# Expert weight stream of a two-layer trunk: VectorE's side steps placed further back, a later second scatter, and the first eight weight pieces loaded early

## The reference, cut to what matters

```python
def swiglu(h, w1, w3, w2):
    return jnp.matmul(jax.nn.silu(jnp.matmul(h, w1)) * jnp.matmul(h, w3), w2)

def moe_swiglu(h, router, w1, w3, w2):
    logits = jnp.einsum('bld,de->ble', h, router, preferred_element_type=F32)
    top_v, top_i = lax.top_k(logits, TOP_K)                       # TOP_K = 2, N_EXPERTS = 8
    wts = jax.nn.softmax(top_v, axis=-1)
    gates = jnp.sum(jax.nn.one_hot(top_i, N_EXPERTS, dtype=F32) * wts[..., None], axis=-2)
    y = jnp.zeros_like(h)
    for e in range(N_EXPERTS):
        y = y + gates[..., e:e + 1].astype(h.dtype) * swiglu(h, w1[e], w3[e], w2[e])
    return y
```

## Time and profile before

| | us |
|---|---|
| median of 3 runs | 2085.04 |
| lowest, highest | 2084.29, 2087.69 |
| the profiled execution | 2080.13 |
| its span, first to last instruction | 2078.3 |

### The profile page before, as it was taken

One profiled execution on the slowest core, in us unless ns is written; L12 is line 12 of the kernel. 1 busy time (PEld: TensorE's weight loads), 2 busy tenths in 40 slices (PEclk: granted clock), 3 DMA queues, 4 the chain that ended last, 5 costly groups with the idle time before them and its releaser, 6 DMA issues.

```text
span 2078.3 us, 34564 instructions
## 1 busy us (share of the span) xinstructions
PE 1870.7 (90%) x15227; PEld 1214.5 (58%) x15227; DVE 1169.4 (56%) x1387; ACT 346.5 (17%) x615; POOL 72.8 (4%) x60
## 2 busy tenths in 40 slices
PE   4999999986799999697899996779999999999997
PEld 1334556985444444243546586476868768687684
DVE  2130154764533222122133476489989998998996
ACT  2001144002232222111012402211010000100000
POOL 0032000001000000000050000000000000000000
PEclk9999999757899999799999976789999999999999
DMA  9631210001245544321122100099999999999993
GB/s 341 260 122 61 81 41 0 1 1 41 106 144 196 199 145 182 122 97 46 41 81 101 41 1 20 21 367 411 412 412 410 401 410 396 402 408 397 410 400 139
DMA packets 112803, 408.88 MB, mean 197 GB/s; under 512 B 13880, under 2 KB 20728, under 8 KB 106512
## 3 DMA queue, kind: packets, MB, share of 16 engines
q1 hardware_dynamic: 110608, 405.60, 50.4%
q10 hardware_dynamic: 2048, 1.02, 0.2%
HBM read 405.55 MB, written 1.05 MB: 196 GB/s over the span
## 4 chain that ended last, share of the span: by engine, by line
PE 71%; DVE 18%; issue 4%; DMA 3%; ACT 2%; DVEq 1%; SPq 1%; POOLq 0%; PEldq 0%; ACTq 0%; POOL 0%; PEld 0%
DVE ARENA L1641 12%; PE PS L1259 11%; PE PS L602 11%; PE PS L600 8%; PE PS L1241 6%; PE PS L814 5%; PE PS L1523 4%; PE PS L1526 4%; PE PS L1525 4%; PE PS L1178 3%; PE PS L447 2%; PE PS L1071 2%; PE PS L1545 1%; DMA ARENA<-in_ada_w 1%; PE PS L1503 1%
## 5 line engine op out<-in xcount | busy, mean ns | idle before, releaser
L1641 DVE TENSOR_TENSOR ARENA<-ARENA 128x2816 bf16<-128x2816 f32 (+1 forms) x192 | 581.5, 3083 | 5.6 <-DMA ARENA<-in_moe_w 3.7
L1523 PE MATMUL PS<-ARENA 128*128 128x96 bf16 x2816 | 375.5, 209 | 41.8 <-DVE ARENA L1641 37.0
L1526 PE MATMUL PS<-ARENA 128*128 128x96 bf16 x2816 | 374.7, 208 | 0.1
L1525 PE MATMUL PS<-ARENA 128*128 128x96 bf16 x2816 | 374.7, 208 | 0.0
L1523 PEld LDWEIGHTS PS<-ARENA 128*128 128x128 bf16 x2816 | 279.4, 99 | 56.5 <-DVE ARENA L1641 48.8
L1525 PEld LDWEIGHTS PS<-ARENA 128*128 128x128 bf16 x2816 | 279.6, 99 | 5.3 <-issue 5.3
L1526 PEld LDWEIGHTS PS<-ARENA 128*128 128x128 bf16 x2816 | 279.4, 99 | 0.5 <-issue 0.3
L1545 PE MATMUL PS<-ARENA 128*96 128x512 bf16 x1056 | 237.6, 384 | 3.1 <-DVE ARENA L1641 3.1
L602 PE MATMUL PS<-ARENA 128*128 128x512 f32 (+1 forms) x608 | 237.4, 536 | 2.4 <-ACTq L397 2.4
L1259 PE MATMUL PS<-ARENA 128*128 128x512 bf16 x1056 | 232.4, 381 | 2.4 <-DVE ARENA L1291 2.4
L380 DVE TENSOR_TENSOR ARENA<-ARENA 128x4096 bf16<-128x4096 f32 (+1 forms) x26 | 91.4, 3522 | 226.8 <-ACT ARENA L374 226.8
(11 more groups left out here) (222 smaller groups left out, 1574.6 us busy)
## 6 DMA issues: line engine op xcount, KB each, us to landing
ARENA<-in_moe_w SPq DMA_DIRECT2D x128, 1408.0 KB, 13.4
ARENA<-in_moe_w SPq DMA_DIRECT2D x48, 1536.0 KB, 16.3
ARENA<-in_ada_w SPq DMA_DIRECT2D x24, 2048.0 KB, 7.8
ARENA<-in_ffn_w SPq DMA_DIRECT2D x15, 2048.0 KB, 7.8
ARENA<-in_w_in SPq DMA_DIRECT2D x12, 2048.0 KB, 8.0
ARENA<-in_moe_w SPq DMA_DIRECT2D x16, 1024.0 KB, 16.7
ARENA<-in_w_out SPq DMA_DIRECT2D x8, 1024.0 KB, 5.6
ARENA<-in_w_in SPq DMA_DIRECT2D x4, 1024.0 KB, 6.1
```

The source lines that it names most:

```text
L1523: pe.matmul(out, hi[:, f:f + P], HEH[:, k, :], start=k == 0 and b % 4 == 0, stop=False, skip_group_check=True)
L1525: pe.matmul(out, hi[:, f:f + P], HEL[:, k, :], start=False, stop=False, skip_group_check=True)
L1526: mm = pe.matmul(out, lo[:, f:f + P], HEH[:, k, :], start=False, stop=k == KC - 1, skip_group_check=True)
L1641: dve.tensor_tensor(WLO[q % NSLOT][:, 0:n], RAW[q % NSLOT][:, 0:n], WHI[q % NSLOT][:, 0:n], ALU.subtract).then_inc(S("m_lo"), 1)
```

## The change

The weight slots and the small tiles of the experts get other places in the arena, so that six of the eight slots lie where nothing is live once the states stage of layer 1 is over. `MIXB`, an output of the states stage, moves away from one of these places. The tiles of the two halves, formerly one tile each with a half index, are now two tiles; shapes and types of the instructions stay.

SP doesn't wait for stage 12 any more but for stage 10 (states). Before its loop it issues pieces 0 to 7 of the first expert: PE opens six slots at the end of its states stage in layer 1 and the last two at the start of `pe_moe_first`. In the loop, SP issues pieces 8 to 23 of an expert and then 0 to 7 of the next; after the last expert of a round it issues pieces 0 to 7 of expert 0 once more, for a round that may follow. With one round those eight loads are used by nobody.

DVE's side steps move: the addition of x = 0 from split 3 to 7, of x = 1 from 6 to 14, the products of the first half from 9 to 11, the one-hot matrices from 12 to 14, the products of the second half from 17 to 18, and the token steps from 20 to 22. PE's scatter of x = 1 moves from after piece 3 to after piece 8. `m_w2_next` is counted by SP and waited for by nobody.

```diff
@@
-        MIXB = A(116, NT, 512)
+        MIXB = A(16, NT, 512)
@@
-        RAW = [A(12 * s, 3 * D) for s in range(NSLOT)]
+        RAW = [A(at, 3 * D) for at in (40, 52, 64, 76, 96, 108, 0, 12)]
+        EARLY = 6
-        WLO = [A(96 + 6 * s, 3 * D // 2).bitcast(BF16) for s in range(NSLOT)]
+        WLO = [A(at, 3 * D // 2).bitcast(BF16) for at in (24, 30, 88, 120, 126, 132, 138, 144)]
...
+        def sp_piece(sp, i, e, q):
+            sp_slot_free(sp, i, q)
+            if q == 16:
+                sp.sem_inc(S("m_w2_next"), 1)
...
+            sp.dma_start(dst, src).then_inc(S(f"m_raw{q % NSLOT}"), 16)
+
         def sp_moe(sp):
             for other in ENG:
-                sp.wait_ge(S(f"{other}_stage_done"), MOE_STAGE)
...
+                sp.wait_ge(S(f"{other}_stage_done"), EARLY_STAGE)
+            for q in range(NSLOT):
+                sp_piece(sp, 0, 0, q)
+            n = sp.value_load(NROUND[0:1, 0:1], min_val=1, max_val=NROUNDS)
+            with sp.Fori(0, n) as c:
+                with sp.Fori(0, N_EXP - 1) as e:
+                    i, later = sp.snap(c * N_EXP + e), sp.snap(e + 1)
+                    for q in range(NSLOT, NPIECE):
+                        sp_piece(sp, i, e, q)
+                    for q in range(NSLOT):
+                        sp_piece(sp, i + 1, later, q)
+                for q in range(NSLOT, NPIECE):
+                    sp_piece(sp, c * N_EXP + N_EXP - 1, N_EXP - 1, q)
+                for q in range(NSLOT):
+                    sp_piece(sp, c * N_EXP + N_EXP, 0, q)
@@
         def pe_moe_first(pe):
-            pe.sem_inc(S("m_used"), USED)
+            pe.sem_inc(S("m_used"), NSLOT - EARLY)
@@
-                    if q == 3:
-                        pe.wait_ge(S("m_added"), 4 * i + 2)
-                        pe_scatter(pe, 1)
...
                 for q in range(8, 12):
                     uv_piece(i, q, UBANK)
+                    if q == 8:
+                        pe.wait_ge(S("m_added"), 4 * i + 2)
+                        pe_scatter(pe, 1)
@@
-                    if q == 3:
+                    if q == 7:
                         dve_add(dve, 0, 4 * i)
-                    if q == 6:
+                    if q == 11:
+                        dve_hidden(dve, i, 0)
+                    if q == 14:
                         dve_add(dve, 1, 4 * i + 2)
-                    if q == 9:
-                        dve_hidden(dve, i, 0)
-                    if q == 12:
                         dve_onehot(dve, i + 1)
...
-                    if q == 17:
+                    if q == 18:
                         dve_hidden(dve, i, 1)
-                    if q == 20:
+                    if q == 22:
                         dve.wait_ge(S("m_gt"), i + 1)
@@
-        MOE_STAGE = 12
+        EARLY_STAGE = 10
@@
                     stage(pe, L)
+                    if L == 1 and stage == pe_states:
+                        pe.sem_inc(S("m_used"), USED - NSLOT + EARLY)
```

More of the change, by code:

```diff
@@ L1334, in trunk @@
         HALF, HB = D_FF // 2, FC // 2
-        RAW = [A(12 * s, 3 * D) for s in range(NSLOT)]
+        RAW = [A(at, 3 * D) for at in (40, 52, 64, 76, 96, 108, 0, 12)]
+        EARLY = 6
         WHI = [v.bitcast(BF16).rearrange("p (n two) -> p n two", two=2)[:, :, 1] for v in RAW]
-        WLO = [A(96 + 6 * s, 3 * D // 2).bitcast(BF16) for s in range(NSLOT)]
[L1338 to L1343, removed]
+        WLO = [A(at, 3 * D // 2).bitcast(BF16) for at in (24, 30, 88, 120, 126, 132, 138, 144)]
+        UA = [A(150, HB * SLOTS), A(154.125, HB * SLOTS)]
+        AEH = [v.bitcast(BF16).rearrange("p (n two) -> p n two", two=2)[:, :, 1] for v in UA]
+        AEL = [A(158.25, HB * SLOTS // 2).bitcast(BF16), A(36, HB * SLOTS // 2).bitcast(BF16)]
+        HEH, HEL = [A(at, KC * SLOTS // 2).bitcast(BF16).rearrange("p (k s) -> p k s", k=KC) for at in (38.0625, 94)]
+        PG = [A(39.5625, SLOTS), A(95.5, SLOTS)]
         MOLD = BYTES
@@ L1467, in sp_slot_free @@
                 sp.wait_ge(S("m_used"), USED * i + USED + 3 * (q // 4 - 2) + q % 4 + 1)
+        def sp_piece(sp, i, e, q):
+            sp_slot_free(sp, i, q)
+            if q == 16:
+                sp.sem_inc(S("m_w2_next"), 1)
+            if q < 16:
+                half, k = q // 8, 2 * (q % 4)
+                w = t["moe_w3" if q % 8 >= 4 else "moe_w1"][0, bass.ds(e, 1), P * k:P * k + 2 * P,
+                                                           HALF * half:HALF * half + HALF]
+                src = w.rearrange("a (k p) n -> p (a k) n", p=P)
+                dst = RAW[q % NSLOT][:, 0:2 * HALF].rearrange("p (k n) -> p k n", k=2)
+            else:
+                c0, c1 = YBLOCKS[q - 16]
+                w = t["moe_w2"][0, bass.ds(e, 1), P * c0:P * c1, :]
+                src = w.rearrange("a (c p) n -> p (a c) n", p=P)
+                dst = RAW[q % NSLOT][:, 0:D * (c1 - c0)].rearrange("p (c n) -> p c n", n=D)
+            sp.dma_start(dst, src).then_inc(S(f"m_raw{q % NSLOT}"), 16)
@@ L1540, in y_piece @@
                     half, s0 = c // HB, SLOTS * (c % HB)
-                    ah, al = AEH[:, half, s0:s0 + SLOTS], AEL[:, half, s0:s0 + SLOTS]
+                    ah, al = AEH[half][:, s0:s0 + SLOTS], AEL[half][:, s0:s0 + SLOTS]
                     for h in range(2):
@@ L1604, in act_silu_u @@
                 act.wait_ge(S("m_full"), FULL * i + 6 * half + n + 1)
-                act.activation(UA[:, half, SLOTS * b0:SLOTS * b1], B(UBANK + n)[:, 0:SLOTS * (b1 - b0)],
+                act.activation(UA[half][:, SLOTS * b0:SLOTS * b1], B(UBANK + n)[:, 0:SLOTS * (b1 - b0)],
                                ACT.Silu).then_inc(S("m_u"), 1)
```

9 lines of the change are left out of this document (4 added, 5 removed).

## The result

| | before | after |
|---|---|---|
| median (runs) | 2085.26 us (6) | 2075.97 us (6) |
| lowest, highest | 2082.90, 2087.69 | 2069.56, 2076.70 |
| the profiled execution, its span | 2080.13, 2078.3 | 2076.63, 2074.9 |

The ratio is 0.9949, with a 95% interval from 0.9935 to 0.9963: faster by about 10 us, where 2070 was forecast with a range of 2059 to 2080. A second set of runs of the same changed kernel gave 0.9952 (0.9939 to 0.9966).

The account below looks back on a forecast made before the run. The DVE-PE loop, 86.9 an expert, was taken as the bound; the change would leave the stream's 85.6, started 13.3 us earlier. Span 2078.3 becomes 2063.0 (-15.3); off the median 2069.7, said as 2070, range 2059 to 2080.

Parts of the forecast that it names:

- early loads' cost in stage 11: What the early-loaded pieces take from stage 11: bounded by 0 and 2 us, taken as 0.
- stall of the addition: DVE's stall ahead of an expert's first addition, waiting for PE's scatter, goes wholly; experts fall from 86.9 us to 85.6.
- PE alone, one expert: PE's matmuls, scatters, transposes, gather and turn in one expert, summed from rows to 82.7 us.
- stream, later experts: Weight-load stream, with small interruptions, takes 85.6 us an expert and becomes the bound.
- piece 8 lands: First reload of slot 0 lands 6.2 us after its issue, at 1376.8, putting the stream 13.3 us ahead.
- pauses of the stream: After the restart, freed slots' landings are never over 0.5 us behind the stream's pace, about 1 us in all.
- from there to PE's end: From the last real landing to PE's last w2 matmul: 12 us, y16 starting when split 16 is done.
- eight loads: Unneeded loads behind the last expert hold the stream 28.5 us longer, to 2060.0, with the store queued behind them.
- rival D: PE waits in the experts lower its granted clock to 1.2 GHz; losing 8 us an expert gives 2092; 3%.
- A (the stall only moves): DVE's stall moves to the first products, experts stay at 86.9 us; span -2.4, time 2082.6; 7%.
- B: Loads don't get ahead because SP is held up or the first slots are late; span -3, 2082 us; 3%.
- C (hidden tail): Store isn't behind the eight last loads, or interruptions are fewer; 2062 to 2067 us; 20%.

Follow-up runs that it names:

- partial loads: Changed kernel with only 256 of the 1408 or 1024 columns of each weight piece loaded, the first eight pieces whole: one run, 2048.6 us.

## Why the prediction was right, and where its sum was off

The direction and the median within the range were right, and so was the cause of the gain: DVE's wait for the scatter held the loop at 86.9, and moving the additions takes it away. What the new bound is was wrong. By the prediction's steps, all times behind the first split:

| step | forecast | measured |
|---|---|---|
| first split | unmoved | 8.1 later in this profile, not by the change |
| early loads' cost in stage 11 | 0 | 0.1 or less |
| stall of the addition | gone, replaced by the stream | gone: DVE waits 19.6 for loads, PE doesn't wait for DVE |
| PE alone, one expert | 82.7 | 85.3 |
| stream, later experts | 85.6 | 85.1 to 86.6 |
| piece 8 lands | 14.3 | 15.3 |
| pauses of the stream | 1 | about 4.7 |
| last real landing | 669.0 | 673.7 |
| from there to PE's end | 12 | 13.2 |
| PE's end | 681.0 | 686.9 |
| eight loads | 28.5 | 27.7 |
| end of the span | 700.5 | 704.4 |
| change of the part behind the split | -15.3 | -11.4 |

**The step that failed** is PE's price: "So every wait has at least a piece to spare, and the loop falls to PE's **82.7**, below the stream's 85.6." The first half of that came true behind the first expert, where the smallest lead of a split is 2.4 us. The price did not: PE takes 85.3 beside the full stream without waiting for a split. The sum had the 2.5 at the turn, and its matmuls are right to 0.2. It had nothing for the stops inside pieces (1.6 an expert), and put the half-clock stretches at nothing with "The granted clock was 0.99 over the loop, so PE's rows hold"; they and delays too short to be listed cost about 1.2 an expert. So PE never had the 2.9 of slack against the stream on which the forecast and rival D count. "y16 starts when split 16 is done" held in before (0.1 us behind it), but in the last expert of after PE starts y16 2.6 behind the split. PE's end is therefore its own sum, not the last landing plus 12: from the end of piece 1 of expert 0 it is 88.4, six times 85.3 and what is left of expert 7. That the stream's 85.6 stood in the forecast for a loop of 85.3 is luck.

The forecast of the stream was off too. "A freed slot's landing 6.2 later is then never more than 0.5 behind the stream's own pace, in all about 1 us": the 6.2 was the shortest landing of before, the first reload took 7.1, and the next three 7.7 to 8.3. And the replay had full clock at the start of expert 1, where a half-clock stretch delayed the first freed slots: uv0 ended 96.4 behind the first split, not 94.1. The stream's head start over before, read at piece 9 of each expert, is 12.4, then 8.4, 7.9, and stays at 7 to 8. By the trace these 4 us cost nothing at the end: what the head start had to do was to keep the splits ahead of PE, and the smallest lead of a split is 2.4 us in after and 1.0 in its second profile. There it falls from 6.1 in the second expert to 1.0 in the last, as a stream of 85.7 beside a PE of 85.3 must make it; with more experts the stream would bind after all.

The reading of the earlier trace rows in the prediction, "PE loses 28.3 us to late splits", counts the turns in; less than half of it is late splits.

**What was right by compensation.** The forecast of -15.3 was laid on the median, which hid that before's profile had a short head. The measured medians moved by 9.3 (and 0.9952 of 2086.26 is 10.0), less than 11.4 and 15.3; the difference of 1 to 2 us to the profiles is inside what the head does.

**The rivals.** A (the stall only moves): DVE's idle time moved to loads, not to the products, and no split is late by it; refuted. B: refuted, SP issued at 1305.4 and the six pieces had landed 38 us ahead of the first split. C (hidden tail): near the truth in its mechanism. Removing the eight loads gains nothing measurable, since PE's end came so late that they were 0.9 us in the store's way, not 3. D (granted clock): happened in small. After has seven half-clock stretches between the first split and PE's end where before has six, most at an expert's start, each some 1.3 to 1.5 us for PE. They count in full, as PE has no slack, but none made an expert lose the 5 us that D needed. The price of D was also added up wrongly: a loss of 8 an expert is 5.1 above the slack of 2.9 assumed there, 41 us over eight experts, so 2111 and not 2092.

## What to carry to other kernels

Sum the work of each engine and of the DMA over one turn of the loop before reading its waits: with three chains within 5% of each other, removing one stall is worth only the distance to the next chain. The price of a chain must be taken beside the traffic that it will run with: PE took 80.0 an expert with few loads and, with no wait for its data, 85.3 beside the full stream. Before a listed wait is called a wait for data, compare the time at which that data was ready with the time of its use; at the turns of before and after they were 5 to 11 us apart. A wait in an in-order queue costs by what the engine behind it has in hand at that moment, not by its length in the list: 32 us of DVE idle cost 1.6 an expert here, 25 us in another place nothing. And a load stream that is made to start early needs free slots to stay ahead: with all slots full it stands still, and restarts at the pace at which they come free.

## What the runs showed of the hardware

- A load of 1408 KB with nothing ahead of it in the queue landed 5.9 to 7.1 us after its issue, each of the three reloads behind piece 8 of after, with one or two ahead, 7.7 to 8.3; in a full queue loads landed 3.46 apart.
- PE stood still for 2.3 to 3.8 us, once 4.9, at each turn of the experts' loop in all kernels with whole loads, with its split ready 4.9 us or more before it went on; with partial loads (DMA share 0.31) for 0.4 or less.
- Six loads (8448 KB) beside compute had no effect on PE, DVE and ACT: the same 112 matmuls took 27.10 and 27.06 us with a DMA share of 0.73 and 0.17.
- The granted clock of PE fell to 1.2 GHz for 3.4 us behind idle times of 2.1 to 2.6 us, and not behind all of them: at the seven turns of after, of 2.3 to 2.6 each, five times. The first 370 us of one and the same program differed by 6 us between two executions, with 20.5 and 34.1 us at the lower clock.
